# Keys, queries and values of a decoder step projected by seven half-size products per column block

## The chip, the cores and the metric

One NeuronCore of a Trainium2 chip runs the whole kernel in one launch. The metric is device time in microseconds from the first to the last instruction of an execution; three executions of the kernel before are shown.

## The reference

One inference step of a two-layer decoder for 1024 prompt tokens and 8 decode tokens, model width 1024, float32. Layer 0 is a pooling mixer and a convolutional FFN. Then one shared set of keys and values is projected, `kv = rms_norm(x, g_kv) @ w_kv`, and the queries of layer 1, `q = rms_norm(x, g_attn) @ w_q`. There are three head groups with windows 128, 512 and 2048 and dilations 1, 4 and 16, of 8 heads of 64 columns each, so nine sets of 512 columns. Keys and queries are then normed head by head, `rms_norm(k, k_gain)`, and the first 16 columns of each head are rotated; values are taken as they are. The rows of keys and values are outputs too. Dilated window attention, an output projection and a second FFN follow.

## The kernel before, in words

The five engines work through queues of their own, written out in order in the file, and wait for each other by semaphores. Matmuls take float32 operands split in a high part that the matmul reads exactly and a low part: `hi*hi + hi*lo + lo*hi`, three matmuls for one.

Order of the work: pooling mixer (`pe_pool`), up projection of FFN 0 (`pe_ffn`), down projection (`pe_down`), projection of keys, queries and values (`pe_project`), attention (`pe_attention`), output projection (`pe_merge`), FFN 1. The two FFNs already use seven half-size products (Strassen's scheme in Winograd's form): the names P1 to P7, T1 to T4, B11, B21, B22, e1, u2, U3 and c11 to c22 belong to it. Four quarter blocks of each operand are added up first, seven products are made, and the quarters of the result come out of partial sums: a product lies in two PSUM banks, ScalarE copies a running sum (`e1` into other banks, `u2` and `u3` to SBUF), and later products are accumulated on it.

The projection (`sp_project`, `act_project`, `dve_project`, `pool_project`, `pe_project`, lines 1861 to 2166) is direct. For each group g and each u (0 keys, 1 queries, 2 values) it goes over nine tiles of tokens, eight of 128 and one of the decode tokens, in a loop. For a tile PE runs 8 row blocks x 3 matmuls whose stationary operand is a 128x128 block of x (tiles `xh`, `xl`) and whose moving operand is 512 columns of weights (`wq`), into one of three PSUM banks. The decode tile takes 16. The weights of a set come in four pieces of 512 KB; ScalarE scales them by the norm's gain into the high part (L1946) and VectorE makes the low part (L1948). For keys and queries ScalarE squares the tile, VectorE reduces it per head, ScalarE takes the root, VectorE refines and scales (`newton`, L2051), GpSimd multiplies by the gain and rotates (L2105 to L2113), SP stores the rows. For values VectorE scales (L2033) and SP stores.

Beside the values of each group, GpSimd and VectorE make the scores of the 8 decode tokens: GpSimd loads the cached keys of token s into one of two buffers (L2087) and its query row (L2091), multiplies (L2123), and VectorE reduces (`sample_scores`, L2062). A buffer is loaded again when its reduction is done. The last two reductions of the last group stand in the attention's queue (`LAST_SCORES`).

The last tiles are followed by the first turns of the attention (`pe_first_turns`), whose queries and keys come back from DRAM. The attention begins with scores on PE, maxima on VectorE (L2577) and exponentials on ScalarE (L2735). The x tile stays in SBUF all the while.

Of the kernel before, what the change touches and what calls it, by code (L numbers as in the profile page):

```python
# [17 lines left out]
P = 128  # L18
D = 1024
# [41 lines left out]
def build(nc, a, o):  # L61

    with ExitStack() as ctx:
# [12 lines left out]
        rx = ExitStack()  # L76
        ua = sb("ua", [P, 2 + N], F32, rx)
# [9 lines left out]
        acc = sb("acc", [P, N])  # L87
        sq = sb("sq", [P, 2, 16 + N])
# [4 lines left out]
        gT = sb("gT", [P, 6 * KC])  # L93
        sel = sb("sel", [NS * HIST, 4, NS])
# [18 lines left out]
        xh = sb("xh", [P, KC, N], F32R, r1)  # L113
        xl = sb("xl", [P, KC, N], F32R, r1)
# [92 lines left out]
        wq0 = sb("wq0", [P, 4, 2, QW], F32R, r2)  # L207
        sb("over_w1", [P, 2048], F32, r2)
        wq1 = sb("wq1", [P, 4, 2, QW], F32R, r2)
        sb("over_u", [P, 36], F32, r2)  # L210
        wq2 = sb("wq2", [P, 4, 2, QW], F32R, r2)
        sb("over_g", [P, 32], F32, r2)
        kn = sb("kn", [P, 3, QW], F32, r2)
        rot = sb("rot", [P, 2, 9, 16], F32, r2)
        hg = sb("hg", [P, 2, HD], F32, r2)
        hs = sb("hs", [P, 5, HEADS], F32, r2)
        r2.close()
        wq = [t[:, i] for t in (wq0, wq1, wq2) for i in range(4)]
        r2 = ExitStack()
        sb("over_wp1", [P, 2 * KC, HW], F32, r2)  # L220
        maskf = sb("maskf", [P, 3, P], F32, r2)
        qt0 = sb("qt0", [P, QW], F32, r2)
        kvt0 = sb("kvt0", [P, 2 * QW], F32, r2)
# [4 lines left out]
        identb = sb("identb", [P, P], BF16, r2)  # L228
        r2.close()
        mask = (masks[:, 0:QW], masks[:, QW:QW + 2 * P], masks[:, QW + 2 * P:QW + 4 * P])  # L230
        skc = (acc[:, 0:QW], acc[:, QW:2 * QW])
        sqb = (rb[:, 0:QW], rb[:, QW:2 * QW])
# [15 lines left out]
        sc = utail[:, :, :, :].rearrange("p q c j -> p (q c j)")[:, 0:192]  # L248
# [7 lines left out]
        srow = sq[0:NS, 1, 512:512 + QW]  # L256
# [26 lines left out]
        set0 = sem("set0")  # L283
# [9 lines left out]
        tl_p, in_gb = sem("tl_p"), sem("in_gb")  # L293
# [7 lines left out]
        split_hi, split_lo = sem("split_hi"), sem("split_lo")  # L301
# [3 lines left out]
        class Split:  # L305

            def __init__(self, sq, acc):
                self.sq = sq
                self.acc = acc
                self.hi = self.lo = 0  # L310
# [8 lines left out]
        ct_out, cv_out = sem("ct_out"), sem("cv_out")  # L319
# [40 lines left out]
        pj_h, pj_l = sem("pj_h"), sem("pj_l")  # L360
        pj_pe = sem("pj_pe")
        pj_n = sem("pj_n")
        pj_half = sem("pj_half")
        pj_a = sem("pj_a")
        pj_sq, pj_rt = sem("pj_sq"), sem("pj_rt")
        pj_s = sem("pj_s")
        pj_v = sem("pj_v")
        pj_r = sem("pj_r")
        pj_x, pj_k = sem("pj_x"), sem("pj_k")
# [12 lines left out]
        in_mask, in_new, in_diag = sem("in_mask"), sem("in_new"), sem("in_diag")  # L382
# [20 lines left out]
        y_a, y_v, y_out = sem("y_a"), sem("y_v"), sem("y_out")  # L403
# [154 lines left out]
        def sp_start(sp):  # L558
# [19 lines left out]
            sp.dma_start(acc[:, 0:D], a["g_pool"][0].partition_broadcast(P)).then_inc(in_gb, 16)  # L578
# [5 lines left out]
        def sp_pool_tails(sp):  # L584
            sp.wait_ge(tl_p, 2)
            sp.dma_start(o["pool_prompt"][0, 0], rb[P - HIST:P, 0:D]).then_inc(tl_out, 16)
            sp.dma_start(o["pool_sample"][0, :, HIST - 1, :], sq[0:NS, 1, 0:D]).then_inc(tl_out, 16)
# [161 lines left out]
        def pool_start(g):  # L749
            nc.gpsimd.memset(ones[:, :], 1.0).then_inc(set0, 1)  # L750
            nc.gpsimd.memset(rtmp[:, 3, :], 1.0).then_inc(set0, 1)

            g.wait_ge(in_gb, 16)
# [5 lines left out]
        def act_start(act):  # L759
# [9 lines left out]
            act.wait_ge(set0, 2)  # L769
# [14 lines left out]
            act.wait_ge(wp_in, 16)  # L784
# [226 lines left out]
        def sp_ffn(sp, L, S, begin, done):  # L1011
# [52 lines left out]
            for n in range(9, NSTEPS):  # L1064
# [3 lines left out]
                if n == NSTEPS - 8:  # L1068
                    sp_conv_tails(sp, L)
                if n == 11:  # L1070
# [372 lines left out]
        def sp_conv_tails(sp, L):  # L1443
# [4 lines left out]
            sp.dma_start(o["conv_prompt"][L, 0].rearrange("c (q n) -> c q n", q=4), rows(0, 2)).then_inc(cv_out, 16)  # L1448
            sp.dma_start(o["conv_sample"][L, :, 1, :].rearrange("c (q n) -> c q n", q=4), rows(2, CT)).then_inc(cv_out, 16)
# [215 lines left out]
        def act_split_quad(act, S, Sx, i, d):  # L1665
# [8 lines left out]
            nc.scalar.activation(quadrant(xh, i, d), quadrant(x, i, d), ACT.Copy).then_inc(split_hi, 1)  # L1674
# [5 lines left out]
        def dve_split_quad(v, S, Sx, i, d):  # L1680
            v.wait_ge(split_hi, Sx.hi + KH * QUADS[i] + d + 1)
            nc.vector.tensor_tensor(quadrant(xl, i, d), quadrant(x, i, d), quadrant(xh, i, d).bitcast(F32),
                                    ALU.subtract).then_inc(split_lo, 1)

        def pool_quads(g, Sx):
            for i in (3, 4, 5, 6):
                for d in range(KH):
                    j, h = KH * QUADS[i] + d, TARGETS[i][1]
                    if j in (0, 4):
                        continue  # L1690
# [3 lines left out]
                    nc.gpsimd.tensor_tensor(half(acc, h), half(acc, h), half(sq[:, d % 2, 0:N], h), ALU.add).then_inc(split_acc, 1)  # L1694

# [4 lines left out]
        def act_downs(act, S):  # L1700
            for n in range(7, NSTEPS):
# [8 lines left out]
                if S.L == 0:  # L1710
                    split_quads_at(act, S, n, act_split_quad)

        def split_quads_at(e, S, n, split_quad):
            for i in (3, 4, 5):
                d = n - NP * (i + 1) - 3
                if 0 <= d < KH:
                    split_quad(e, S, split[1], i, d)

        def dve_downs(v, S):
            for n in range(7, NSTEPS):  # L1720
# [10 lines left out]
                if S.L == 0:  # L1731
                    split_quads_at(v, S, n, dve_split_quad)
# [1339 lines left out]
```

## Time and profile before

| | us |
|---|---|
| median of 3 runs (lowest, highest) | 2135.53 (2135.42, 2136.53) |
| span of the profiled execution | 2134.4 |
| PE busy | 2106.5 (99%) |
| VectorE (DVE) busy | 1533.9 (72%) |
| ScalarE (ACT) busy | 967.6 (45%) |
| GpSimd (POOL) busy | 559.0 (26%) |

An execution's own device time isn't listed beside its profile; the span is what the profiler saw of it. Busy shares are averages over stages with different limits. PE is at work almost throughout, so a time is read as the number of matmuls times the spacing at which they start; a record's own duration is longer than that spacing, since matmuls are pipelined.

### The profile page before, as it was taken

How to read it: one execution, taken by the hardware profiler on the slowest of the kernel's cores; microseconds unless marked ns; L12 is line 12 of the kernel's file. 1: busy time of each engine (PE TensorE's matmuls, PEld its weight loads, DVE VectorE, ACT ScalarE, POOL GpSimd, SP SyncE). 2: the span in 40 equal slices, each digit the busy share in tenths (PEclk: the TensorE clock that was granted, in tenths of full speed). 3: DMA queues.
4: the chain of work that ended last, by engine and by line, in shares of the span. 5: the costliest groups of instructions: out<-in, count | busy, mean ns of one | idle time of the engine just before them, and what ended most of it. 6: DMA issues, size and time to landing. Idle time of an engine off the chain costs nothing.

```text
span 2134.4 us, 42632 instructions
## 1 busy us (share of the span) xinstructions
PE 2106.5 (99%) x15883; PEld 1958.0 (92%) x15883; DVE 1533.9 (72%) x2321; ACT 967.6 (45%) x1797; POOL 559.0 (26%) x780
## 2 busy tenths in 40 slices
PE   7999999999999999999999999999999999999998
PEld 7999999999999987777777776899999999999998
DVE  4888888888755767457465588878888888875544
ACT  4655545555544542123122255645554554553342
POOL 1002232223100135455455301640213323311000
PEclk8999999999999999999999999999999999999999
DMA  6236777888986532432532785221567788899664
GB/s 195 90 95 161 199 198 193 207 193 234 300 276 195 181 110 85 158 100 84 169 114 93 228 243 159 70 90 55 155 191 196 193 210 195 198 291 303 194 209 142
DMA packets 237758, 371.02 MB, mean 174 GB/s; under 512 B 23687, under 2 KB 120615, under 8 KB 235734
## 3 DMA queue, kind: packets, MB, share of 16 engines
q1 hardware_dynamic: 196806, 258.73, 36.9%
q0 software_dynamic: 34960, 104.33, 22.0%
q10 hardware_dynamic: 5864, 6.25, 0.9%
q8 instruction: 81, 1.33, 0.3%
q14 instruction: 47, 0.39, 0.1%
HBM read 297.75 MB, written 168.07 MB: 218 GB/s over the span
## 4 chain that ended last, share of the span: by engine, by line
PE 95%; DVE 2%; ACT 1%; issue 0%; DMA 0%; POOL 0%; ACTq 0%; SPq 0%; DVEq 0%; POOLq 0%
PE ps L1255 42%; PE ps L1358 20%; PE ps L2164 6%; PE ps L2166 6%; PE ps L2165 6%; PE ps L2364 2%; PE ps L2434 2%; PE ps L2466 1%; PE ps L2447 1%; PE ps L424 1%; PE ps L2397 1%; PE ps L866 1%; PE ps L490 1%; PE ps L2426 1%; PE ps L2158 1%; PE ps L2159 1%
## 5 line engine op out<-in xcount | busy, mean ns | idle before, releaser
L1255 PE MATMUL ps<-hT,w 128*128 128x258 f32 x2752 | 458.2, 283 | 0.0
L1255 PEld LDWEIGHTS ps<-hT,w 128*128 128x128 f32 x2752 | 384.8, 189 | 0.5 <-ACT acc L1189 0.4
L1255 PE MATMUL ps<-lT,w 128*128 128x258 f32 x1376 | 276.3, 282 | 0.0
L1255 PE MATMUL ps<-hB,w 128*128 128x258 f32 x1344 | 229.3, 282 | 0.0
L2164 PE MATMUL ps<-wq,xh 128*128 128x512 f32 x576 | 227.6, 395 | 0.7 <-DVE wq L1948 0.7
L2166 PE MATMUL ps<-wq,xl 128*128 128x512 f32 x576 | 227.4, 395 | 0.0
L2165 PE MATMUL ps<-wq,xh 128*128 128x512 f32 x576 | 226.9, 394 | 0.0
L1255 PEld LDWEIGHTS ps<-lT,w 128*128 128x128 f32 x1376 | 213.3, 189 | 0.0
L1358 PE MATMUL ps<-gdh,wda 128*128 128x258 f32 x1184 | 198.8, 283 | 0.0
L1358 PE MATMUL ps<-gdh,wdb 128*128 128x258 f32 x1152 | 193.5, 284 | 0.1
L1255 PEld LDWEIGHTS ps<-hB,w 128*128 128x128 f32 x1344 | 191.0, 189 | 0.0
L1358 PEld LDWEIGHTS ps<-gdh,wda 128*128 128x128 f32 x1184 | 166.7, 190 | 0.3
L1358 PEld LDWEIGHTS ps<-gdh,wdb 128*128 128x128 f32 x1152 | 161.7, 189 | 0.9 <-issue 0.2
L1609 POOL DMA_DIRECT2D wsum<-in_w_down x44 | 24.0, 553 | 486.2 <-DMA stage<-in_w_up 417.4
L1200 ACT ACTIVATE w<-sq 128x1024 fp32r<-128x1024 f32 x84 | 88.8, 1058 | 111.0 <-PE ps L1255 99.9
L1612 POOL DMA_DIRECT2D wsum<-in_w_down x88 | 80.2, 1088 | 222.0 <-DMA stage<-in_w_up 173.0
L2164 PEld LDWEIGHTS ps<-wq,xh 128*128 128x128 f32 x576 | 108.2, 188 | 29.7 <-DVE wq L1948 4.1
L1255 PE MATMUL ps<-lB,w 128*128 128x258 f32 x672 | 135.4, 283 | 0.0
L2166 PEld LDWEIGHTS ps<-wq,xl 128*128 128x128 f32 x576 | 108.0, 188 | 25.5
L2165 PEld LDWEIGHTS ps<-wq,xh 128*128 128x128 f32 x576 | 108.2, 188 | 25.1
L1358 PE MATMUL ps<-gdl,wda 128*128 128x258 f32 x592 | 119.0, 282 | 0.0
L1507 DVE SCALAR_TENSOR_TENSOR cb<-ub,cwT,cb 128x1024 f32<-128x1024 f32 x88 | 112.5, 1279 | 7.6 <-ACT cb L1742 7.6
(350 smaller groups left out, 4714.7 us busy)
## 6 DMA issues: line engine op xcount, KB each, us to landing
stage<-in_w_up SPq DMA_DIRECT2D x176, 256.0 KB, 3.7
wsum<-in_w_down POOLq DMA_DIRECT2D x132, 256.0 KB, 5.3
gs<-cb SPq DMA_DIRECT2D x44, 516.0 KB, 7.0
stage<-wsum SPq DMA_DIRECT2D x88, 256.0 KB, 2.9
tsum<-gs POOLq DMA_DIRECT2D x66, 258.0 KB, 7.7
tsum<-gneg POOLq DMA_DIRECT2D x66, 258.0 KB, 8.4
stage<-in_w_down SPq DMA_DIRECT2D x58, 256.0 KB, 3.2
stage<-in_w_kv SPq DMA_DIRECT2D x24, 512.0 KB, 4.3
```

The costliest lines, as they stand in the source:

```text
L424: mm = pe.matmul(ps[:, bank0 + c, 0:NW], w, m[:, c * NW:(c + 1) * NW], start=(i == 0), stop=(i == len(parts) - 1))
L1200: nc.scalar.activation(out, src, ACT.Copy).then_inc(f_hi, 1)
L1255: mm = pe.matmul(ps[:, bank + c, 0:HB], w, m[:, c * HB:(c + 1) * HB], start=(first and i == 0), stop=(i == len(parts) - 1), skip_group_che ...
L1358: mm = pe.matmul(ps[:, 2 * d + c, 0:HB], w, m[:, c * HB:(c + 1) * HB], start=(i in FRESH and p == 0 and j == 0), stop=(last and j == 2), s ...
L1507: nc.vector.scalar_tensor_tensor(out=c[:, 0:T], in0=u[:, t:t + T], scalar=w, in1=c[:, 0:T], op0=ALU.mult, op1=ALU.add).then_inc(f_conv, 1)
L1609: q.dma_start(dst, src).then_inc(sums_in, 16)
L1612: q.dma_start(dst, src, accum_op=ALU.add, max_dma_last_dim=4 * N).then_inc(sums_in, 16)
L2164: pe.matmul(out, xh[:, k, tok], W, start=(k == 0), stop=False)
L2165: pe.matmul(out, xh[:, k, tok], Wt, start=False, stop=False)
L2166: mm = pe.matmul(out, xl[:, k, tok], W, start=False, stop=(k == KC - 1))
L2364: mm = pe.matmul(ps[:, bank0 + n, 0:NW], w, m[:, c * NW:(c + 1) * NW], start=(i == 0), stop=(i == len(parts) - 1))
L2434: mm = pe.matmul(ps[:, b + odd, at:at + P], qT[part, s % 2, hp * P:(hp + 1) * P], kT[part, slot, hp * P:(hp + 1) * P], start=False, stop=True,
```

## The change

The projection takes the form of the FFNs. Each of the nine sets is one step `n` (groups in the order 1, 2, 0): x's prompt part is cut in four quarters (512 rows of the model width x 512 tokens), the set's weights in four (512 rows x 256 columns). Sums of x's quarters (S1 to S4) are made once, on GpSimd; sums of the weights (T1 to T4) in each step, on VectorE. For that x itself is overwritten: it is spilled to DRAM and comes back in the attention. A result block (c11, c22, c12, c21) holds four token tiles x 256 columns in two banks, tokens on the partitions, and is drawn, normed, rotated and stored whole.

- `pe_project`: seven products of 48 matmuls of 256 columns a step, order T1, T2, B21, T3, next step's B11, B22, T4 (last step: T4 before B22); decode tokens in 4 x 8 matmuls of 256 columns; two 512-wide matmuls before the first T1 that open banks 2 and 3.
- `act_project`: scaling of the raw weights in place (16 instructions of 256 columns a step), 7 high parts of 1024, copies e1, u2, u3, c11, c21 of 1024, squares and roots per block.
- `dve_project`: 4 weight sums, 7 low parts, c22 and c12 drawn from PSUM with an addition, per-block reduction, `newton` and scaling; the reductions of the sample scores.
- `pool_project`: per block one multiplication of 1024 columns and four operations for the rotation; then the sample scores; the last step's c12, S and c21 scaled by GpSimd.
- SP: quarters of x spilled, first weights and tables loaded during the down projection; x loaded back at steps 10 to 17 of the attention; the new rows loaded at step 3.
- The former passes that made `xh` and `xl` of all of x, the first pieces of weights and `act_next_tiles` go. Some semaphores are merged.

The core of the diff:

```diff
@@ pe_project
+            def product(n, b):
+                pe.wait_ge(pj_l, nth(n, b))
+                if n == 0 or (n == 1 and b == "B11"):
+                    x_ready(b)
+                hi, lo = xq[PARTNER[b]]
+                w = wslot(n, b)
+                for t in range(KH):
+                    out = ps[:, BANK[b] + t // 2, t % 2 * CW:(t % 2 + 1) * CW]
+                    tok = slice(t * P, (t + 1) * P)
+                    for k in range(KH):
+                        cols = slice(k * CW, (k + 1) * CW)
+                        pe.matmul(out, hi[:, k, tok], w[:, 0, cols], start=(b in ("B11", "T1") and k == 0 and t % 2 == 0), stop=False,
+                                  skip_group_check=True)
+                        pe.matmul(out, hi[:, k, tok], w[:, 1, cols], start=False, stop=False, skip_group_check=True)
+                        mm = pe.matmul(out, lo[:, k, tok], w[:, 0, cols], start=False, stop=(k == KH - 1),
+                                       skip_group_check=True)
+                mm.then_inc(pj_pe, 1)
...
+            for n in range(LASTP + 1):
+                wait(pe, pj_cs, 2 * n)
+                product(n, "T1")
...
+                pe.wait_ge(pj_cp, 5 * n + 1)
+                product(n, "T2")
+                samples(n, "B21")
+                product(n, "B21")
+                samples(n, "T3")
+                pe.wait_ge(pj_cp, 5 * n + 2)
+                product(n, "T3")
+                if n < LASTP:
+                    samples(n + 1, "B11")
+                    pe.wait_ge(pj_cp, 5 * n + 3)
+                    product(n + 1, "B11")
+                    samples(n, "B22")
+                    pe.wait_ge(pj_cs, 2 * n + 1)
+                    product(n, "B22")
+                    pe.wait_ge(pj_cp, 5 * n + 4)
+                    product(n, "T4")
+                else:
+                    pe_first_turn(pe, 0)
+                    samples(n, "B22")
+                    pe.wait_ge(pj_cp, 5 * n + 4)
+                    product(n, "T4")
+                    pe_first_turn(pe, 1)
+                    pe.wait_ge(pj_cs, 2 * n + 1)
+                    product(n, "B22")
@@ dve_project, one step, second half (first half: T3's sum, then the previous step's c12, S, c21 between low parts)
+                dve_lo(v, n, "B22")
+                if not last:
+                    dve_weights_sum(v, n + 1, "T1")
+                    dve_weights_sum(v, n, "T4")
+                if normed:
+                    dve_mean(v, n, "c11")
+                    dve_sample_add(v, n, 0)
+                    dve_normed(v, n, "c11")
...
+                dve_c22p(v, n)
...
+                else:
+                    dve_values(v, n, "c22")
+                    sample_scores(v, gi, 0)
+                    sample_scores(v, gi, 1)
+                if last:
+                    dve_masks(v)
+                    v.wait_ge(at_tp, 1)
+                    nc.vector.tensor_copy(qT[:, 0, :], ps[:, 6, :]).then_inc(at_tc, 1)
+                else:
+                    dve_lo(v, n + 1, "T1")
+                    dve_weights_sum(v, n + 1, "T2")
+                if not normed:
+                    sample_scores(v, gi, 2)
+                    sample_scores(v, gi, 3)
+                dve_sample_add(v, n, 1)
+                if last:
+                    v.wait_ge(at_tp, 2)
+                    nc.vector.tensor_copy(kT[:, 0, :], ps[:, 6, :]).then_inc(at_tc, 1)
+                    sample_scores(v, gi, 4)
+                    sample_scores(v, gi, 5)
+                dve_c12p(v, n)
+                if not last:
+                    dve_lo(v, n + 1, "T2")
+                    if not normed:
+                        sample_scores(v, gi, 4)
+                        sample_scores(v, gi, 5)
@@ pool_project, one step
+                if n and PSTEPS[n - 1][1] != 2:
+                    for name in ("c12", "S", "c21"):
+                        turned_heads(n - 1, name)
+                if u != 2:
+                    turned_heads(n, "c11")
+                    turned_heads(n, "c22")
+                    continue
+                load_keys(gi, 0)
+                load_keys(gi, 1)
+                q.wait_ge(*rows_stored(n - 1, "S"))
+                load_query(gi, 0)
+                load_query(gi, 1)
@@ sp_attention
+                if s == 3:
+                    sp_new_rows(sp)
...
+                if 10 <= s < 10 + KC:
+                    sp.dma_start(x[:, s - 10, :], xsp[s - 10]).then_inc(x_spq, 16)
```

`dve_c22p` and `dve_c12p` are one addition of two banks and a saved sum each; `dve_mean` is the reduction per head, `dve_normed` the scaling. In the values steps `sample_scores` waits for GpSimd's multiplication of that token (`sm_p`), and GpSimd's next load into a buffer waits for the reduction (`sm_r`), as before.

## Rows read from the trace of the kernel before

**Rows 1.** Busy time by stretches: us, each engine (instructions), PE's clock, DMA, GB/s.

```profile
121.00:513.00 392.00, 392.00 (x3267) 392.00 (x3266) 331.64 (x391) 208.37 (x296) 96.41 (x143) 1.00 0.72 187
575.00:755.00 180.00, 179.98 (x1488) 179.51 (x1489) 109.64 (x159) 84.34 (x148) 20.88 (x20) 1.00 0.70 220
766.70:1206.20 439.50, 438.82 (x1899) 342.55 (x1898) 257.50 (x577) 100.23 (x191) 231.35 (x345) 1.00 0.37 120
1222.00:1260.00 38.00, 36.59 (x388) 27.58 (x386) 33.27 (x53) 19.50 (x86) 0.00 (x0) 1.00 0.89 275
```

**Rows 2.** Chain of waits, projection: start us, us, what.

```profile
776.12 1.80 PE ps L2152 x18
...
1201.84 0.44 PE ps L2380 x4
1202.28 0.44 PE ps L2384 x4
```

**Rows 3.** Instructions with tile wq: durations in ns (min/median/max), first and last start.

```profile
L2164 PE MATMUL ps<-wq,xh x576: 387/393/505, 766.7 to 1201.0; 128*128 128x512 f32 x192
...
L1948 DVE SCALAR_TENSOR_TENSOR wq<-stage,gT,wq x72: 740/751/2126, 762.6 to 1160.4; 128x512 fp32r<-128x512 f32 x72
```

**Rows 4.** Groups of instructions by shape: busy us, mean ns, idle before.

```profile
L1090 DVE TENSOR_TENSOR w<-sq,w 128x1024 fp32r<-128x1024 f32 x84 | 102.3, 1218 | 2.3 <-ACT w L1200 2.3
...
L1200 ACT ACTIVATE w<-sq 128x1024 fp32r<-128x1024 f32 x84 | 88.8, 1058 | 111.0 <-PE ps L1255 99.9 <-DVE sq L1104 7.8 <-DVE sq L1474 3.4
...
L2577 DVE TENSOR_REDUCE sg<-ps 128x4 f32<-128x1024 f32 x14 | 17.1, 1220 | 2.1 <-PE ps L2434 2.1
...
L637 DVE RECIPROCAL hs<-hs 128x8 f32<-128x8 f32 x48 | 9.7, 203 | 13.2 <-ACT hs L1985 13.2
```

**Rows 5.** Timelines of VectorE and GpSimd, last key tiles of the first group.

```profile
866.68 4.04 DVE L1948 SCALAR_TENSOR_TENSOR wq<-stage,gT,wq 128x512 fp32r<-128x512 f32 x4
861.23 1.29 POOL L2105 TENSOR_TENSOR kn<-kn,hg 128x512 f32<-128x512 f32 x1 [2.42 <-DVE kn L2051]
862.59 0.46 POOL L2107 TENSOR_TENSOR sq<-kn,rot 128x128 f32<-128x128 f32 x1
...
866.84 1.73 POOL L2105 TENSOR_TENSOR kn<-kn,hg 128x512 f32<-128x512 f32 x1 [2.68 <-DVE kn L2051]
868.65 0.79 POOL L2107 TENSOR_TENSOR sq<-kn,rot 128x128 f32<-128x128 f32 x1
```

**Rows 6.** Timeline of GpSimd, values of the second group.

```profile
1025.11 1.06 POOL L2091 DMA_DIRECT2D rb<-qs  x2 [0.85 <-DMA qs<-kn]
1031.94 1.29 POOL L2123 TENSOR_TENSOR acc<-acc,rb 128x512 f32<-128x512 f32 x1 [5.77 <-DMA rb<-qs]
1034.37 0.56 POOL L2087 DMA_DIRECT2D acc<-in_cache_kv_w  x1 [1.14 <-DVE utail L2062]
...
1040.13 1.29 POOL L2123 TENSOR_TENSOR acc<-acc,rb 128x512 f32<-128x512 f32 x1 [1.09 <-DMA rb<-qs]
```

**Rows 7.** Timeline of GpSimd, values of the third group and the attention's start.

```profile
1178.36 1.28 POOL L2123 TENSOR_TENSOR acc<-acc,rb 64x512 f32<-64x512 f32 x1 [6.08 <-DMA rb<-qs]
...
1199.16 1.29 POOL L2123 TENSOR_TENSOR acc<-acc,rb 64x512 f32<-64x512 f32 x1
...
1203.58 0.55 POOL L2087 DMA_DIRECT2D acc<-in_cache_kv_w  x1 [3.13 <-DVE utail L2062]
...
1212.20 1.26 POOL L2123 TENSOR_TENSOR acc<-acc,rb 64x512 f32<-64x512 f32 x1 [6.19 <-DMA rb<-qs]
```

**Rows 8.** Timeline of PE and VectorE from the last product to the first maximum.

```profile
1206.26 0.40 PE L2426 MATMUL ps<-masks,identb 128*128 128x256 bf16 x2
...
1208.26 0.67 DVE L2577 TENSOR_REDUCE st<-ps 128x4 f32<-128x512 f32 x1
```

**Rows 9.** Busy time by stretches, start-up (columns as in rows 1).

```profile
20.00:28.00 8.00, 5.92 (x49) 5.52 (x49) 6.74 (x15) 5.05 (x13) 0.00 (x0) 0.50 1.12 319
28.00:44.00 16.00, 15.60 (x85) 15.49 (x86) 7.29 (x8) 3.81 (x5) 6.72 (x2) 0.61 0.31 97
```

More of the change, by code:

```diff
@@ L1694, in pool_quads @@
                     nc.gpsimd.tensor_tensor(half(acc, h), half(acc, h), half(sq[:, d % 2, 0:N], h), ALU.add).then_inc(split_acc, 1)
+                for d in range(KH):
+                    if i >= 4:
+                        pool_x_sum(g, {4: "S3", 5: "S2", 6: "S4"}[i], d)
         def adds_after(S, i):
@@ L1858, in store_result @@
                 cols = slice((KH * D1 + d - 1) * P, (KH * D1 + d + 1) * P)
-                e.dma_start(o["y_sample"][:, 0, cols], yst[0:NS, 8, cols]).then_inc(y_out, 16)
+                e.dma_start(o["y_sample"][:, 0, cols], yst[0:NS, 8, cols]).then_inc(out_w, 16)
         MT = [P] * 8 + [NS]
-        K0 = 5
-        def pj_src(u, part, g, later):
+        CW = QW // 2
+        GORDER = (1, 2, 0)
+        PSTEPS = [(g, u) for g in GORDER for u in range(3)]
+        LASTP = len(PSTEPS) - 1
+        ORDER_IN = ("T1", "T2", "B21", "T3", "B11", "B22", "T4")
@@ new lines, in build @@
+        ORDER_LAST = ("T1", "T2", "B21", "T3", "T4", "B22")
+        PARTNER = {"B11": "A11", "T1": "S1", "T2": "S2", "B21": "A12", "T3": "S3", "B22": "S4", "T4": "A22"}
+        BANK = {"B11": 0, "B21": 0, "T1": 4, "B22": 4, "T2": 2, "T3": 2, "T4": 2}
+        XPARTS = ("A11", "S1", "S2", "S3", "A12", "S4", "A22")
+        XSUMS = ("S3", "S1", "S2", "S4")
+        UNITS = ("c11", "c22", "c12", "S", "c21")
+        BIG = ("c11", "c22", "c12", "c21")
+        TAIL_FIN = 7 * KH
+        UNIT0 = 8
@@ new lines, in sp_spill_quad, with bidx, stores, rows_stored @@
+        def sp_spill_quad(sp, i, d):
+            D1, h = TARGETS[i]
+            sp.wait_ge(f_xa, KH * i + d + 1)
+            sp.dma_start(half(xsp[KH * D1 + d], h), quadrant(x, i, d)).then_inc(x_spq, 16)
+        def bidx(n, name):
+            return 4 * n + BIG.index(name)
+        def stores(n):
+            g, u = PSTEPS[n]
+            return 2 if g == 2 and u != 1 else 1
+        def rows_stored(n, name):
+            if name == "S":
+                return (rows_s, 16 * sum(stores(j) for j in range(n + 1)))
+            i = bidx(n, name)
+            return (rows_out[i % 3], 16 * sum(stores(j // 4) for j in range(i % 3, i + 1, 3)))
```

999 lines of the change are left out of this document (634 added, 365 removed).

## The prediction

> **What bounds the kernel now.** I read the page first: TensorE (PE) is busy 99% of the span and holds 95% of the chain that ended last, VectorE 72%, ScalarE 45%, GpSimd 26%. Then the busy time by stretches [rows 1]: in the projection, from 766.70 to 1206.20 us, PE is busy for 438.82 of 439.50 us at a granted clock of 1.00 (the 2.4 GHz level), VectorE for 257.5, GpSimd for 231.4, ScalarE for 100.2. The chain of waits shows PE's small extra work there [rows 2]. So PE alone bounds the stretch: what is taken from its stream is gained, unless the new order makes it wait, which it hardly does now.
>
> **The products.** Before, one set of keys, queries or values of one head group takes 8 token tiles x 8 x 3 products of 512 columns and 16 for the decode tokens: 208; nine sets make 1872. The rows agree: 576 instructions of each of the three lines of the prompt tiles [rows 3], which leaves 9 x 16 for the decode tokens. The stretch from 766.66 to 1206.26 us, less 1.80 for the sums of squares and 0.88 for the first turns [rows 2], is 436.9 us, or 233.4 ns for each. After, one set takes seven products of 4 token tiles x 4 x 3 matmuls of 256 columns (336) and 32 for the decode tokens: 368; nine sets make 3312. None of 256 columns with this pattern stands in the trace. The up projection's, 258 wide, one weight load each, come every 392.0/3267 = 120.0 ns; the down projection's every 180.0/1488 = 121.0 [rows 1]. The bounds are half of 233.4 (116.7: 386.5 us) and 121.0 (400.8 us). I take the line through 258 columns at 120.0 and 512 at 233.4, which gives 119.1 at 256: 394.5 us. Saved: 42.4. Two dummy 512-wide matmuls that open banks 2 and 3 cost 0.5; the sums of squares and first turns stay. Net **-41.9** (-49.9 to -35.6).
>
> The Trainium skill (TensorE: Matmul & The Clock Gate, section Back-to-back issue gap) gives N/2.4 + 2.5 ns for an isolated gap, 109.2 ns at 256 columns; the sum would be 33 us lower by it, but it gives 110.0 at 258 where the trace has 120.0, so the measurement decides.
>
> **The clock of one step.** Let 0 be the end of the previous set's T4 on PE. A product is 48 x 0.119 = 5.7 us, a decode part 8 x 0.119 = 0.95. T1 ends at 5.7, T2 at 11.4, B21 at 18.1, T3 at 24.8, the next B11 at 31.5, B22 at 38.1, T4 at 43.8. PE needs c22 out of banks 4 and 5 at 32.4 (before B22), c12 at 43.8 (before the next T1).
>
> **VectorE and GpSimd in a step of keys or queries.** A two-input pass over 128x1024 is 1.22 us, a reduction 1.22 [rows 4]; back to back each counts 0.08 less, since a record overlaps the next. Fifteen passes with both inputs in SBUF (7 low parts, 4 weight sums, 4 scalings by 1/norm) 17.1, four reductions 4.6, two additions from PSUM 2.3, small ones (reciprocal 0.20 and its like) 4.0, the decode unit and its additions 3.2: 31.2 us of 43.8. GpSimd: a 512-wide multiplication takes 1.29, a 128-wide one 0.46 [rows 5]; on the line through both a unit of 1024 is 2.5 + 2 x 0.46 + 2 x 0.75, about 5.0, four are 19.9, with the decode unit 22.7. Neither fills the step by itself. But they get in each other's way: four VectorE passes, 0.75 each alone [rows 3], 2.8 in a row, took 4.04 us while GpSimd's multiplication beside them went from 1.29 to 1.73 and the next operation from 0.46 to 0.79 [rows 5]. After every scaling VectorE's next low part finds GpSimd in a multiplication of 2.5. I lay the queue out in order: square of c12 on ScalarE at 3.2 (after c21 and the copy e1, 1.06 each [rows 4]), c12 scaled at 7.8, low part of T3 held to 11.4, c21 scaled at about 18, low part of B11 held to 21.5, c22 drawn at 31-32 (limit 32.4), c12 at 43 to 45 (limit 43.8). What is late is thus late by 0 to 1.5. The six such steps cost 0 to 12 together; I take **+3**, near the lower end, since the limit is only just met.
>
> **The sample scores** hang on another cycle: GpSimd loads cached keys and the query row, multiplies, VectorE reduces, and only then may GpSimd load into that buffer again. From the last of the first four loads to the first multiplication is 6 us (1026.17 to 1031.94), from a key load to its use 5.8 (1034.37 to 1040.13) [rows 6]. Counted from the first multiplication x: reduction 1 is done at x+5.5, 3 at x+13.8, 5 at x+22.0; the trace's last group has 20.8 from the first multiplication to the sixth's start [rows 7], where this count has 20.0. Now GpSimd starts only after c12, the decode unit and c21 of the queries are turned: c21 is scaled at 18, its unit of 5.0 shares the port, so the loads start at 24 and x = 24 + 2.2 (four issues of 0.55) + 6 = 32. In the values steps of the first two groups VectorE's queue has reductions 0 to 3 ahead of the pass that draws c12: 32 + 13.8 + 1.6 = 47.6 against 43.8. Behind it PE's T1 of the next step waits. About 4 each, **+8** (0 if the turning ends by 20; 9 each if at 29).
>
> **The last step** has T4 before B22, PE through at 38.6 with the two turns. VectorE's queue has the masks, both copies of the turns and reductions 0 to *5* ahead of c12; behind that stands the first maximum of the attention, for which ScalarE and then PE wait. No ScalarE scaling of new weights stands in the way here, so x is about 30: reduction 5 at 52, c12 at 53.3, maximum 0 right behind it. Before, the maximum came 2.0 us after PE's last product (1206.26 to 1208.26 [rows 8]); that would be at 40.6. So the attention starts 12.7 later than PE could let it, **+12.5** (2 if GpSimd were free at 12; 16 if at 26). PE's stall between the turns is inside this figure.
>
> **Rest.** At the start: spills and first weights move into the down projection's SP queue behind waits that VectorE meets before the next low part anyway; half of x's sixteen block sums on GpSimd have the last 32 us of it. T1, T2 and B21 of the first set find their parts 2 to 5 us early by the same laying-out: 0 to 3. In the attention x returns, eight loads of 516 KB on SP at steps 10 to 17; steps 2 to 7 already carried more and PE was busy 36.59 of 38 us there [rows 1]. SP stands at step 3 for the last rows' stores, with the next tiles loaded ahead. And PE sits idle some 9 us before the attention: in the start-up, where it idled too, the clock was 0.50 and then 0.61 over 16 us that were 15.6 busy [rows 9]. Together 0 to 6; I take **+2**.
>
> **The sum.** Span 2134.4 - 41.9 + 3 + 8 + 12.5 + 2 = 2118.0; the median of the runs shown, 2135.5, stands 1.1 above that span, so 2119.1 us, 0.8% faster.
>
> **Rivals.**
> *A, all is hidden.* PE stays full as in the FFN, whose seven products wait for nothing (the stretch of 392 us is busy 392.00). For it: each engine's sum is below 43.8. Against it: the six reductions ahead of the last c12, whose cycle the trace shows. 2135.5 - 41.9 + 2 = 2096 us.
>
> *B, slower: the port makes VectorE and GpSimd one engine.* If their passes excluded each other wholly, nothing of either beside the other, a keys or queries step would take 31.2 + 22.7 = 53.9 us, 10.1 over PE's. Six steps: 60.6 instead of 3, 2177 us. It decides from 3.2 us a step on: from there the kernel is slower than before. For it: the 4.04 us against 2.8 [rows 5]. Against it: reductions and PSUM additions (6.9) and the small ones (7.2) ran beside GpSimd undisturbed, and where both wanted SBUF the two together still took less than their sum, 2.8 + 2.4.
> The Trainium skill (SBUF — State Buffer, section Who interferes with whom) says that a VectorE instruction with two SBUF inputs and a GpSimd instruction that reads SBUF hold a shared port exclusively. By that rule, the trace agrees for two-input passes and gives no ground for the rest of VectorE's queue, so B keeps a small chance.
>
> *C, long trips.* The last trip before the attention took 8.6 us from the key load (1203.58) to the multiplication (1212.20) [rows 7], 2.8 more than the 5.8. With the large stores and weight loads in the same queues all might: two trips in each values step (+5.6 twice), three in the last (+8.4): +19.6, 2139 us.
>
> **How the numbers follow.** Forecast 0.50, A 0.15, B 0.09, C 0.11; 0.08 lies between A and the forecast, 0.07 between it and no change. Within 0.2% of the time before (2131.2 to 2139.8) is about what a measurement of this kernel can tell from none. There fall 0.07 of C and 0.04 of the last: 0.11. Slower are B and 0.02 of C: 0.11. Faster are the forecast, A, what lies between them, 0.02 of C and 0.03 of the last: 0.78. The range reaches from the middle of A to C; about 0.08 of A, B and the slow end of C are left out, 0.19: 2098 to 2139.
>
> **What would show it.** The stretch of the projection at about 420 us where 395 + 3 is PE's work. PE's rows 256 wide at 119 to 120 ns; if 117 or 121, the first term is off. PE's T1 after a values step waiting about 4 us for VectorE's c12; GpSimd's sixth multiplication of the last group about 50 us after the last step's start, and the first maximum directly behind c12. No wait longer than 1.5 us in keys and queries steps. If PE has no wait before the attention, A is right and my reading of VectorE's order is wrong; if it waits in every step for c22 or c12, B; if the loads land 8 us after issue, C.

## The result, and the profile after

The kernel with the change takes 2150.33 us (median of 4 runs, 2149.32 to 2151.09), the one before, on the same chip, 2135.48 (4 runs, 2134.94 to 2136.53): 1.0072 of the time, 95% interval 1.0058 to 1.0086. It is 0.7% slower, 31 us from the forecast and on its other side.

The page after: span and busy time of each engine, then the granted clock in 40 slices. PE is at work for 34 us less than before, in a span 15 us longer.

```profile
span 2149.3 us, 44749 instructions
...
PE 2072.2 (96%) x17309; PEld 2018.1 (94%) x17325; DVE 1609.6 (75%) x2155; ACT 1079.0 (50%) x1953; POOL 621.6 (29%) x679
...
PEclk8999999999999999999999899999999999999999
```

Busy time by stretches (columns as in rows 1). First the kernel before: from the first product of the projection to the first scores, and from there to the output product. Then the kernel after, the same two.

```profile
766.66:1206.26 439.60, 438.92 (x1901) 342.59 (x1899) 257.54 (x577) 100.27 (x191) 231.35 (x345) 1.00 0.37 121
1206.26:1400.40 194.14, 188.96 (x1907) 142.34 (x1906) 161.02 (x296) 109.30 (x439) 53.65 (x60) 1.00 0.51 157
```

```profile
766.85:1216.50 449.65, 406.91 (x3342) 403.72 (x3340) 324.18 (x411) 208.36 (x335) 260.04 (x222) 0.96 0.38 120
1216.50:1414.90 198.40, 188.58 (x1892) 143.60 (x1906) 161.96 (x297) 107.42 (x437) 63.07 (x69) 0.99 0.57 177
```

The projection, forecast at about 420, takes 449.65 us. PE was full in it before (438.92 of 439.60) and now stands for 43, at a mean clock of 0.96. The attention costs 4.3 more, the rest next to nothing: the output product starts at 1414.91 instead of 1400.44, 14.5 later, and the span is 14.9 longer. What PE waited for between 760 and 1450 us (line, by whom it was released: us in total, times, longest):

```profile
PE ps L2560 <- DVE stage L2315: 17.2, 3, 8.2
PE ps L2579 <- DVE knS L2320: 14.8, 8, 3.1
PE ps L2832 <- DVE qT L2441: 10.8, 1, 10.8
PE ps L2838 <- DVE qT L3016: 3.6, 1, 3.6
```

L2560 are products: T1 waits for the pass that draws c12. L2579 are the decode tokens' matmuls, which wait for the addition that empties their bank, L2832 the first key tile's turn behind the copy of the query's, L2838 the next key's. From each of its three longest stands (8.2, 8.0 and 10.8 us) PE comes back at half clock, 0.50 by the first two rows (the 1.2 GHz level, columns as in rows 1); for 4 to 5 us it starts about half as many matmuls as at 2.4 GHz.

```profile
922.04:926.00 3.96, 3.96 (x18) 3.96 (x19) 1.76 (x2) 0.00 (x0) 2.94 (x3) 0.50 0.47 132
...
1208.10:1213.00 4.90, 4.90 (x23) 4.90 (x24) 1.12 (x2) 0.00 (x0) 3.40 (x4) 0.50 0.58 186
...
1213.00:1217.00 4.00, 4.00 (x35) 3.75 (x35) 1.86 (x4) 0.00 (x0) 2.42 (x3) 0.99 0.51 153
```

From the first matmul behind such a wait to a mark 96 matmuls on (T1 and T2: 11.5 us where nothing disturbs them) it takes 13.5 and 14.1 us in the two values steps: 2.0 and 2.6 lost to the clock. Behind the turn it is 2.2, and behind one wait of 3.0 in a queries step (56 matmuls in 8.18 us, elsewhere 6.7) 1.5: 8.3 in all. Another wait of 3.1 cost no clock. The last version below gives the work: PE is busy for 398.5 us there, of which 1.6 are slow clock behind its one longer wait. So 396.9 of work at full clock + 17.2 + 14.8 + 10.8 + 8.3 = 448.0 of the 449.65. The 1.7 left is not attributed; an estimate for it is that a record outlasts the spacing by 0.16 us (0.28 against 0.12), so that each of the twelve stops costs that much beside its idle time.

### The profile page after: what moved, and what is told of

Same layout as the page of the kernel before. It is cut to its first block, busy times and chain, and to the rows that moved or that the text cites. A ratio compares the mean times of both kernels' runs of the same rounds, so it can differ in the third digit from the quotient of the medians.

```text
span 2149.3 us, 44749 instructions
## 1 busy us (share of the span) xinstructions
PE 2072.2 (96%) x17309; PEld 2018.1 (94%) x17325; DVE 1609.6 (75%) x2155; ACT 1079.0 (50%) x1953; POOL 621.6 (29%) x679
## 3 DMA queue, kind: packets, MB, share of 16 engines
q1 hardware_dynamic: 221142, 269.81, 38.6%
## 4 chain that ended last, share of the span: by engine, by line
PE 79%; DVE 8%; POOL 4%; DMA 4%; ACT 3%; issue 2%; SPq 0%; ACTq 0%; POOLq 0%; DVEq 0%
PE ps L1285 40%; PE ps L1388 19%; PE ps L2560 2%; PE ps L2563 2%; PE ps L2562 2%; DMA sqb<-qs 2%; PE ps L2812 2%; PE ps L2875 1%; PE ps L2911 1%; PE ps L445 1%; PE ps L2890 1%; DVE ring L2023 1%; DVE hs L2329 1%; POOL stage L2507 1%; PE ps L2838 1%
## 5 line engine op out<-in xcount | busy, mean ns | idle before, releaser
L2560 PE MATMUL ps<-ring,xhS 128*128 128x256 f32 x560 | 161.6, 289 | 17.2 <-DVE stage L2315 17.2
L2562 PE MATMUL ps<-ring,xhS 128*128 128x256 f32 x560 | 160.8, 287 | 0.0
L2563 PE MATMUL ps<-ring,xlS 128*128 128x256 f32 x560 | 160.5, 287 | 0.0
L2560 PEld LDWEIGHTS ps<-ring,xhS 128*128 128x128 f32 x560 | 109.9, 196 | 17.9 <-DVE stage L2315 17.8
L1388 PE MATMUL ps<-gdl,wda 128*128 128x258 f32 x592 | 119.1, 283 | 0.0
L2562 PE MATMUL ps<-ring,xhA 128*128 128x256 f32 x416 | 117.9, 283 | 0.0
L2560 PE MATMUL ps<-ring,xhA 128*128 128x256 f32 x416 | 117.8, 283 | 0.0
L2563 PE MATMUL ps<-ring,xlA 128*128 128x256 f32 x416 | 117.8, 283 | 0.0
```

What stands on the lines that cost most here:

```text
L1388: mm = pe.matmul(ps[:, 2 * d + c, 0:HB], w, m[:, c * HB:(c + 1) * HB], start=(i in FRESH and p == 0 and j == 0), stop=(last and j == 2), s ...
L2560: pe.matmul(out, hi[:, k, tok], w[:, 0, cols], start=(b in ("B11", "T1") and k == 0 and t % 2 == 0), stop=False, skip_group_check=True)
L2562: pe.matmul(out, hi[:, k, tok], w[:, 1, cols], start=False, stop=False, skip_group_check=True)
L2563: mm = pe.matmul(out, lo[:, k, tok], w[:, 0, cols], start=False, stop=(k == KH - 1), skip_group_check=True)
```

## The experiments

All kernels are edits of the kernel with the change. Each ratio is to runs of the kernel before that were made with it: 2135.9 us for the first four experiments, 2135.4 for the next four, 2135.0 for the last two.

**The addition earlier.** In the chain of waits after, the third decode matmuls of a step stand behind a row of VectorE's passes (chain: start us, us, what):

```profile
989.93 0.96 ACT ring L2018
990.92 1.32 DVE ring L2023
992.24 1.41 DVE xodd L2030
993.65 1.40 DVE xeven L2030
995.04 1.14 DVE hs L2329
996.92 1.11 PE ps L2579 x8
```

Low part of B22, two sums of weights and a reduction are ahead of an addition of 0.40 us, for which nothing is missing but its turn. The edit moves it ahead of all four (in the values steps alike, not shown):

```
                    ...
+                dve_sample_add(v, n, 0)
                 dve_lo(v, n, "B22")
                 ...
                     dve_mean(v, n, "c11")
-                    dve_sample_add(v, n, 0)
                     dve_normed(v, n, "c11")
```

> Only the order of VectorE's queue changes: the addition that empties bank 6 of the decode tokens' first half goes ahead of the low part of B22. Theory (a queue in the wrong order): the eight waits of the decode matmuls for it, 14.8 us together (1.2 to 3.1 each), go, and 1.5 us of slower clock behind one of them; ScalarE's copy that the addition needs is done before B22's low part can start, so nothing takes their place: 2150.3 - 16 = 2134 us (2131 to 2138). Rival (VectorE and GpSimd are full, their shared port makes them one engine): what is taken from this wait comes back as a wait for c22 before B22 or for c12 before T1: 2146 us or more.

2135.69 us (1.0003 of before, 0.9993 to 1.0013): 14.6 less. All eight waits are gone. PE comes to c12 earlier and waits there 3.4 more in all.

```profile
PE ps L2558 <- DVE stage L2315: 20.6, 5, 8.9
PE ps L2830 <- DVE qT L2439: 9.4, 1, 9.4
```

The theory holds: the place of one short instruction cost 14.6 of the 57 us that the change lost against its work.

**Reductions behind c12, values steps.** The core of the edit; 2 and 3 leave their place ahead of c12 too, and 7 follows the low part of the next B11:

```
                     dve_values(v, n, "c22")
-                    sample_scores(v, gi, 0)
-                    sample_scores(v, gi, 1)
...
                     dve_lo(v, n + 1, "T2")
+                        sample_scores(v, gi, 0)
+                        sample_scores(v, gi, 1)
... (the next step)
                         dve_values(v, n - 1, "c12")
+                        sample_scores(v, gi - 1, 2)
                         dve_lo(v, n, "B21")
+                        sample_scores(v, gi - 1, 3)
                         dve_lo(v, n, "T3")
+                        sample_scores(v, gi - 1, 4)
                         dve_values(v, n - 1, "S")
+                        sample_scores(v, gi - 1, 5)
                         dve_values(v, n - 1, "c21")
+                        sample_scores(v, gi - 1, 6)
```

> In the values steps of the first two groups the reductions of the sample scores 0 to 3 go behind the pass that draws c12, and all eight are spread over the next step's queue. Theory: the two waits of T1 for c12, 8.2 and 8.0 us, go, and with them the slower clock behind them (96 matmuls took 2.0 and 2.7 us longer than at 119 ns each): 2150.3 - 21 = 2129 us (2127 to 2134). Rival: VectorE has no room in the next step; the reductions, each waiting for its multiplication, hold up the low parts of B21 and T3 there, and half of it or more comes back: 2140 us.

2146.54 us (1.0051, 1.0035 to 1.0068): 3.8 less instead of 21. The two waits at T1 are gone, but the decode matmuls of the next step wait 8.9 and 6.5 instead of 1.2 each. PE's waits there:

```profile
PE ps L2585 <- DVE knS L2320: 27.6, 8, 8.9
...
PE ps L2566 <- DVE stage L2315: 1.1, 1, 1.1
```

The rival had it: in the first group reduction 0, whose multiplication was done at 910.4 us, now ran at 915.7, and as each load waits for a reduction the whole cycle slid back. VectorE stood 14.1 us of the next 40 for multiplications (six waits, the longest 3.6), with low parts queued behind them.

**Reductions behind the attention's maxima, last step.** Reductions 0 to 3 of this step go from ahead of the masks and the copies:

```
                     nc.vector.tensor_copy(kT[:, 0, :], ps[:, 6, :]).then_inc(at_tc, 1)
-                    sample_scores(v, gi, 4)
-                    sample_scores(v, gi, 5)
+                    sample_scores(v, gi, 0)
                 dve_c12p(v, n)
...
-        LAST_SCORES = {3: NS - 2, 5: NS - 1}
+        LAST_SCORES = {0: 1, 1: 2, 2: 3, 3: 4, 4: 5, 5: 6, 7: 7}
```

> Only the last step: masks and the two copies of the turns stand ahead of every reduction of the sample scores, one reduction ahead of c12, the other seven one by one behind the attention's maxima. Theory: PE's wait of 10.8 us between the turns and the slower clock behind it (2.2) go, and the first maximum comes at about 1206 instead of 1221.2 us of the span: 15 less, of which the attention gives back 0 to 5: 2137 us (2134 to 2141). Rival (the attention's start is held by the queue of SP, which waits at its step 3 for the last rows, and by its loads): 10 or more come back there: 2146 us.

2153.05 us (1.0083, 1.0066 to 1.0100), 2.7 more than with the change: nothing gained. The first maximum did move, from 1221.18 to 1207.0, but one query tile's turn waits 10.5. Timeline of SP's queue in this run (start, us):

```profile
1215.84 0.55 SPq L2699 DMA_DIRECT2D kvt<-kvs  x1
1232.40 0.37 SPq L2140 DMA_DIRECT2D kvs<-stage  x1
...
1235.25 0.37 SPq L2140 DMA_DIRECT2D kvs<-stage  x1
...
1242.63 0.43 SPq L2695 DMA_DIRECT2D qt<-qs  x1
```

SP issues nothing from 1216 to 1232: at its step 3 it stands for c12, S and c21 of the last values, which GpSimd scales behind the eighth multiplication, and the query tile of the next step is behind them. The rival's place was right; its reason is the order of two queues.

**Loads before the turn of c21.** On GpSimd, ahead of the sample scores:

```
-                    for name in ("c12", "S", "c21"):
+                    for name in ("c12", "S") if u == 2 else ("c12", "S", "c21"):
                         turned_heads(n - 1, name)
...
                 load_query(gi, 1)
+                turned_heads(n - 1, "c21")
```

> VectorE's queue stays; GpSimd issues the loads of the first cached keys and query rows before it turns c21 of the queries, not behind it. Theory (the trip of the query row and c21's unit of 9 us in a row set the first multiplication, 38 us after the step's start): the query is issued 7.6 us earlier, c21's unit then lies beside its trip, and the multiplication comes 4 to 5 us earlier in all three values steps. T1's two waits fall from 8 to about 3.5, the slower clock behind them by 1 each, the last c12 comes 4.7 earlier: 2150.3 - 16 = 2134 us (2130 to 2140). Rival (loads are late for the memory's sake, beside stores and weights): the query lands at the same time whenever it is issued: 2148 us or more.

2134.25 us (0.9996, 0.9986 to 1.0006): 16.1 less, as worked out. The timelines of GpSimd show it, the kernel with the change first, second group of scores:

```profile
1035.87 3.35 POOL L2507 TENSOR_TENSOR stage<-stage,hg 128x1024 f32<-128x1024 f32 x1 [1.17 <-DVE stage L2343]
1039.30 1.32 POOL L2510 TENSOR_TENSOR t<-stage,rot 128x128 f32<-128x128 f32 x1
1040.59 1.45 POOL L2511 TENSOR_TENSOR t<-stage,rot 128x128 f32<-128x128 f32 x1
1042.11 1.59 POOL L2513 TENSOR_TENSOR stage<-stage,rot 128x256 f32<-128x256 f32 x1
1043.78 1.60 POOL L2515 TENSOR_TENSOR stage<-stage,t 128x256 f32<-128x256 f32 x1
1045.33 1.09 POOL L2490 DMA_DIRECT2D skb<-in_cache_kv_w  x2
1046.41 1.10 POOL L2494 DMA_DIRECT2D sqb<-qs  x2
1054.84 1.28 POOL L2536 TENSOR_TENSOR skb<-skb,sqb 64x512 f32<-64x512 f32 x1 [7.33 <-DMA sqb<-qs]
```

And this experiment, the first group:

```profile
889.60 1.07 POOL L2494 DMA_DIRECT2D sqb<-qs  x2 [1.62 <-DMA qs<-knS]
...
897.64 1.60 POOL L2515 TENSOR_TENSOR stage<-stage,t 128x256 f32<-128x256 f32 x1
899.20 1.28 POOL L2537 TENSOR_TENSOR skb<-skb,sqb 128x512 f32<-128x512 f32 x1
```

The queries' trip, with the change alone 8.6 us in the first group and 7.3 in the second, now lies beside c21's unit of 9 instead of behind it; the first multiplication of the first group moved from 907.2 to 899.2, more than the 4 to 5 expected. T1's waits fell from 17.2 to 2.3, the one between the turns to 4.4. Against that the decode matmuls' waits rose from 14.8 to 17.9:

```profile
PE ps L2580 <- DVE knS L2320: 17.9, 8, 3.1
PE ps L2561 <- DVE stage L2315: 2.3, 3, 1.1
```

**Two together, and without scores.** The early addition with the loads ahead; and the early addition with the sample scores left out (GpSimd's loop over them is gone, and in `sample_scores`):

```
-            v.wait_ge(sm_p, NS * gi + s + 1)
-            nc.vector.tensor_reduce(sc[0:rows, ...], skc[s % 2][0:rows, :]..., AX.X, ALU.add).then_inc(sm_r, 1)
+            nc.vector.memset(sc[0:rows, ...], 0.0).then_inc(sm_r, 1)
```

> The two edits that each brought back the time before (the addition of the decode tokens' half ahead of B22's low part; the first loads ahead of c21's turn) together. Theory (two separate queues of waits): the 17.9 us of decode waits that the second edit still had go, and some 1.5 of slower clock; PE then reaches c12 earlier and waits there 1 to 3 us more in two steps: 2134.2 - 17 = 2117 us (2113 to 2122). Rival (one shared shortage of VectorE and GpSimd): each edit alone took all that was to be had, together 2130 us or more.

> The early addition, and the sample scores left out: no loads of cached keys and query rows on GpSimd, no multiplications, and in place of each reduction one small memset on VectorE. It bounds what the scores cost in the new order. Theory (the score cycle is all that is left beside a few waits for c12 after keys and queries): from the 2135.7 us with the early addition the waits of 17.4 at T1, 13.6 in the last step and 6.9 of slower clock go: 2098 us (2094 to 2103), which is the rival A of the prediction. Rival (VectorE and GpSimd are too full for PE's shorter step even without scores): 2115 us or more.

Together 2123.59 us (0.9944, 0.9927 to 0.9960): 11.9 less than before, 26.7 of the 30.7 that the two gained singly. T1 waits 12.0 again, in five waits, more than I had put, and the time lies above the range that I gave (2113 to 2122), but below the rival's 2130. Without scores 2099.56 us (0.9838, 0.9821 to 0.9854), as worked out, and 3.6 from the prediction's rival A. This version leaves out the scores' work together with their waits, so it bounds both. Its projection (columns as in rows 1):

```profile
766.85:1169.00 402.15, 398.15 (x3337) 396.35 (x3335) 309.81 (x412) 207.98 (x334) 203.17 (x156) 1.00 0.34 108
```

The one addition and the scores are thus 50.8 of the 57 us that the change lost against its work.

**The last step, mended.** The order of the third experiment, with this on GpSimd behind the *second* multiplication and no longer behind the eighth, and the reductions at `{0: 1, 1: 2, 3: 3, 4: 4, 5: 5, 7: 6, 8: 7}`:

```
+                    if n == LASTP and s == 1:
+                        for name in ("c12", "S", "c21"):
+                            q.wait_ge(*unit_made(LASTP, name))
+                            scale_values(nc.gpsimd, LASTP, name).then_inc(pj_r, 1)
```

> The last step's order as before (masks, the copies and c12 ahead of all but one reduction), and GpSimd scales the last c12, S and c21 of the values behind the second multiplication of the sample scores, not behind the eighth. Theory: the earlier edit gained 14 us at the first maximum and lost it again in one wait of 10.5 for a query tile, because SP stands at its step 3 until GpSimd has scaled these rows (1230 to 1235 us); with the scaling at about 1207 that wait goes: 2153 - 15 = 2138 us (2134 to 2142). Rival (the tile is late because the memory is full at the start of the attention): the wait stays, 2150 us or more.

2144.40 us, with an unusual spread (2139.5 to 2148.7; the profiled span is 2137.7): between the two theories by its median. Of the mechanism the trace is clear: the query tile's wait of 10.5 is gone, and there is a new one of 5.6, scores that wait for a key's copy behind a reduction in VectorE's queue.

**All together, and then each reduction in its place.** First the addition, the loads, the mended last step, and reductions 2 and 3 behind c12. Then the same with each reduction put where its multiplication is done by then; from the first to the second (not shown: in the values steps only 2 stays right behind c12, in the last step 0 goes ahead of the masks and 1 ahead of c12):

```
                         dve_values(v, n - 1, "c12")
+                        sample_scores(v, gi - 1, 3)
                         dve_lo(v, n, "B21")
-                        sample_scores(v, gi - 1, 6)
+                        sample_scores(v, gi - 1, 4)
                         dve_lo(v, n, "T3")
+                        sample_scores(v, gi - 1, 5)
                         dve_values(v, n - 1, "S")
                         dve_values(v, n - 1, "c21")
-                        sample_scores(v, gi - 1, 7)
+                        sample_scores(v, gi - 1, 6)
...
-                    if n == LASTP and s == 1:
+                    if n == LASTP and s == 2:
...
-        LAST_SCORES = {0: 1, 1: 2, 3: 3, 4: 4, 5: 5, 7: 6, 8: 7}
+        LAST_SCORES = {0: 2, 2: 3, 4: 4, 5: 5, 7: 6, 8: 7}
...
                     maxima(i)
-                if i in LAST_SCORES:
-                    sample_scores(v, GROUPS - 1, LAST_SCORES[i])
...
                     outs(i - 2)
+                if i in LAST_SCORES:
+                    sample_scores(v, GROUPS - 1, LAST_SCORES[i])
```

> All of them: the early addition, the loads ahead of c21, the last step's order with the early scaling, and in the values steps the reductions 2 and 3 behind the pass that draws c12. Theory: from the 2117 us expected of the first two, the last step gives 4.4 (between the turns), 5.0 (the next key's turn) and part of the later start, and T1's waits 2 to 5: 2107 us (2102 to 2113), better than both kernels. Rival (attention takes the reductions badly; each waits for its multiplication in the queue of the maxima): 2116 us.

> The same edits as together, with each reduction of the sample scores put where its multiplication is done by then: in the values steps 0 and 1 ahead of c12, 2 behind it, the others one by one behind the next step's passes; in the last step 0 ahead of the masks and 1 ahead of c12, the last rows scaled behind the third multiplication, the other reductions at the end of an attention half step, behind the copies of the turns. Theory: the combination was held by reductions at the head of VectorE's queue (7.3 us before B21, 5.5 and 3.3 for the keys' turns, and their slower clock); these go: 2117.3 - 14 = 2103 us (2100 to 2109), near the 2099.6 without scores. Rival (the queue of the scores needs the time wherever it stands): 2113 us or more.

2117.31 us (0.9913, 0.9896 to 0.9930), 10 above what I expected and 1 above the rival; PE's waits show reductions that head VectorE's queue before their data are there:

```profile
PE ps L2866 <- DVE kT L3015: 8.8, 5, 5.5
PE ps L2578 <- DVE ring L2023: 7.3, 2, 5.3
```

With the placed order 2104.57 us (0.9855, 0.9839 to 0.9872): 1.45% faster than the kernel before, faster than both. The two stretches of this version, and its longest wait:

```profile
766.85:1169.00 402.15, 398.49 (x3339) 396.69 (x3339) 326.18 (x408) 208.84 (x335) 248.78 (x216) 1.00 0.41 132
1169.00:1366.00 197.00, 187.56 (x1878) 142.32 (x1893) 159.62 (x295) 106.10 (x435) 67.47 (x75) 0.98 0.60 183
```

```profile
PE ps L2838 <- DMA qt<-qs: 4.0, 1, 4.0
PE ps L2560 <- DVE stage L2315: 3.1, 3, 2.3
```

VectorE and GpSimd do the same work as in the slow version (326.2 and 248.8 us busy; 324.2 and 260.0 there). Nothing was computed less; the waits went because of the order alone. Of the 50.8 us between the slow version and the one without scores, 45.8 came back with the scores in place.

The wait of 2.3, for the first step's c12, cost clock too. The 96 matmuls from 822.63 on took 13.1 us instead of 11.5, and the stretch behind it shows the granted clock (columns as in rows 1):

```profile
823.00:827.00 4.00, 4.00 (x25) 4.00 (x24) 3.52 (x5) 3.39 (x5) 2.44 (x1) 0.60 0.17 57
```

The 4.0 us is again a stand of SP at its step 3, now for another reason. It issues the stores of the last rows at 1178.8 to 1180.3, but reads them back only when they have landed, and the query tile of the next step is behind that (chain of waits):

```profile
1180.30 9.46 DMA kvs<-stage
```

**The port.** Why GpSimd's unit took 9 us and not 5: the four small operations above, of 0.45 to 0.75 us at their shortest, last as long as the VectorE pass beside them.

```
-            nc.vector.tensor_tensor(raw(n, t), raw(n, one), raw(n, two), ALU.subtract).then_inc(pj_t, 1)
+            nc.vector.tensor_scalar(raw(n, t), raw(n, t), 0.5, None, ALU.mult).then_inc(pj_t, 1)
```

> The changed kernel, with VectorE's 35 differences of weight blocks replaced by a pass of the same size with one input (the block times 0.5): the sum is left out. It asks why GpSimd's small operations took 1.4 to 1.6 us beside these passes, where 0.45 and 0.75 are their shortest. Theory (only a VectorE pass with two inputs in SBUF holds the port): in the turn of c21 the second rotation product and the third, which lie beside two of these passes, fall from 1.45 and 1.59 to 0.5 and 0.8, and the first and the last, beside other two-input passes, stay at 1.32 and 1.60. Rival (any long VectorE pass over SBUF does it, or it is GpSimd's own pace on this pattern): all four stay. The time: 0 to 4 us less, since the first multiplication of the scores comes up to 1.7 us earlier in three steps.

(There are 36 such passes, not 35.) 2141.64 us in a single run, 8.7 less than with the change; this version leaves the sums out. Timeline of GpSimd, the same four operations, and VectorE's two passes beside the middle ones:

```profile
1033.04 1.34 POOL L2510 TENSOR_TENSOR t<-stage,rot 128x128 f32<-128x128 f32 x1
1034.33 0.91 POOL L2511 TENSOR_TENSOR t<-stage,rot 128x128 f32<-128x128 f32 x1
1035.32 1.06 POOL L2513 TENSOR_TENSOR stage<-stage,rot 128x256 f32<-128x256 f32 x1
1036.46 1.61 POOL L2515 TENSOR_TENSOR stage<-stage,t 128x256 f32<-128x256 f32 x1
...
1033.97 0.95 DVE L2030 TENSOR_SCALAR xeven<-xeven 128x1024 f32<-128x1024 f32 x1
1034.85 0.94 DVE L2030 TENSOR_SCALAR xodd<-xodd 128x1024 f32<-128x1024 f32 x1
```

Both theories fall. The first and the last, beside passes with two inputs, stayed (1.34 and 1.61). The middle two went to 0.91 and 1.06, neither to their shortest (0.45, 0.73) nor unchanged: they still last about as long as the pass beside them, but that pass is shorter (0.95 for 1.48). So a VectorE pass with one SBUF input holds GpSimd off too, here one that does 1024 columns in 0.68 us alone, where the difference takes 1.21. The Trainium skill (SBUF — State Buffer, section Who interferes with whom) says that a VectorE pass in a two-port mode, which tensor_scalar can enter, holds the shared port pair for its whole length, while the other engine is fully blocked. This trace agrees, with 0.91 us for an operation of 0.45, if the 0.68 us is that mode. Most of the 8.7 us came elsewhere: the shorter passes stand ahead of the late addition, whose waits fell from 14.8 to 6.5.

## Why the prediction was wrong

The sum of the prediction against the traces, from the projection's start to the output product:

| term | forecast | measured |
|---|---|---|
| PE's work | -41.9 | -42.7 |
| keys and queries steps, and the decode matmuls' wait | +3 | +17.4 |
| values steps of the first two groups | +8 | +20.8 |
| last step and the rest | +14.5 | +17.3 |
| not attributed | 0 | +1.7 |
| sum | -16.4 | +14.5 |

**PE's work: right.** In the placed version PE is busy 398.49 us, which less 1.6 of slow clock and 1.8, 0.9 and 0.5 for the small parts leaves 393.7 for 3312 matmuls, 118.9 ns each. Measured directly, the six steps from the decode matmuls at 879.02 to those at 1142.19, with no wait over 0.5 us, take 263.2 us for 2208 matmuls, 119.2 ns each, where 119.1 was drawn between two rows.

**Keys and queries steps: the failing step.** I laid VectorE's queue out against the limits of c22 and c12 and never listed the third wait of PE in it, the decode matmuls' for `dve_sample_add`. It costs 14.8 in eight steps (values steps too), up to 3.1 each, and 1.5 of clock; c12 took 1.1, once. "No wait longer than 1.5 us in keys and queries steps" is refuted in three of the six (2.3, 3.0, 3.1). For c22 and c12, the limits I did look at, the +3 was near: the placed version has waits of 3.1 and 1.6 of clock. Rival B put waits in these steps, but by another mechanism: the early addition removes them with the port as it is.

**Values steps: right mechanism, wrong size.** T1 waited behind reductions 0 to 3, as written, 8.2 and 8.0 us and not 4 each. The first multiplication came 38.8 and 37.6 us after the step's start, not 32: c21's turn ended at 28 (24 forecast), because its four small operations took 6.0 instead of 2.4 and its multiplication 3.35 instead of 2.5 (the prediction's own line gives 2.4 at 1024 columns). And the queries came 8.6 and 7.3 us after their issue instead of 6. The 6 was read from the second group; the first has 6.9 before. The first group's rows, before and after (timeline of GpSimd):

```profile
887.77 1.29 POOL L2123 TENSOR_TENSOR acc<-acc,rb 128x512 f32<-128x512 f32 x1 [6.85 <-DMA rb<-qs]
...
907.20 1.28 POOL L2536 TENSOR_TENSOR skb<-skb,sqb 128x512 f32<-128x512 f32 x1 [8.57 <-DMA sqb<-qs]
```

From the first multiplication to reduction 3's end it was 13.3 and 14.4 (13.8 forecast). The second omission is the clock: I weighed it for the attention's start alone, and it took 2.0 and 2.6 behind T1's waits.

**Last step: the mechanism right, the size in part by luck.** c12 was drawn by 56.1 us after the step's start (53.3 forecast) behind reduction 5, the first maximum right behind it, at 1221.18; it shows as 10.8 between the turns, 2.2 of clock and 4.3 in the attention. The first multiplication came at 35.1, not 30, and the cycle from it to reduction 5's end took 19.9, not 22.0: two errors that partly cancel. PE's own end in this step, put at 38.6, adds up to 38.0 from the prediction's terms.

**Rivals.** A, everything hidden, is what the order could have given: 2099.6 without scores and 2104.6 with them. C's long trips are there in part: the first trip of each group, from the end of its issue, took 8.6, 7.3 and 6.5 us where the same groups had 6.9, 5.8 and 6.1 before, as part of the values steps; C had 2.8 more, for two or three trips each. B's port is real for single operations, but the engines had room: moved, not shortened, the same instructions let PE run full. The chance of 0.11 for slower was too small for a sum that hung on three hand-laid queues, in which one wait missed is worth 15 us.

## What to carry to other kernels

When the engine that bounds a kernel gets less work, list *every* wait in its stream against the place of its releaser in the other queue, short instructions first: here an addition of 0.4 us behind four long passes cost 14.6 us, net of the 3.4 that PE then waits longer for c12. An instruction that waits for a slow cycle (load, multiply, reduce) belongs where its data are ready by then, neither at the head of a queue that the critical engine needs nor so late that the cycle itself slides; and the loads that start a cycle belong ahead of work that nobody waits for. A wait of 8 us cost 10 here, since the clock came back later than the work.

## What the runs showed of the hardware

- Small GpSimd operations beside VectorE's passes over SBUF took about the pass's length: 1.32 to 1.60 us where 0.45 to 0.75 is their shortest. Beside faster passes of 0.95 they took 0.91 and 1.06.
- After PE had stood for 8.2, 8.0 and 10.8 us its granted clock was 0.50 for the next 4 to 5 us though it was fully busy. After shorter waits it fell or not: in the kernel with the change behind one of 3.0 and not behind those of 3.1 and 2.3, in the placed version behind one of 2.3.
- Two query rows, each spread over 128 partitions, came 8.6, 7.3 and 6.5 us after the end of their issue in the three groups, in the kernel before 6.9, 5.8 [rows 6] and 6.1 [rows 7].
